# Mean squares of queries and keys in a hybrid attention layer: one float32 product replaced by two single-pass fp32r products of a rounded square and its remainder

## The reference, cut to what matters

```python
def _rms(x, w):
    xf = x.astype(jnp.float32)
    y = xf * lax.rsqrt(jnp.mean(xf * xf, axis=-1, keepdims=True) + EPS)
    return (y * w.astype(jnp.float32)).astype(x.dtype)

def _project(x, shift, scale, norm_w, w_in, q_norm_w, k_norm_w):
    h = _rms(x, norm_w) * (1 + scale) + shift
    z = h @ w_in
    q, k, v, g_att, cb, cc, ch, g_conv = jnp.split(z, idx, axis=-1)
    q = _rms(q.reshape(b, n, N_ATT_HEADS, 2, HEAD_DIM), q_norm_w)
    k = _rms(k.reshape(b, n, N_ATT_HEADS, 2, HEAD_DIM), k_norm_w)
    ...
```

## Time and profile before

| what | value |
|---|---|
| three runs, median | 1815.07 us (1813.13 to 1816.41) |
| the profiled execution's own time | 1812.12 us |
| its span, first to last instruction | 1810.3 us |
| mean granted TensorE clock | 0.973 of full speed |
| busy share of the span: PE, DVE, ACT, POOL | 93%, 58%, 44%, 42% |

### The profile page before, as it was taken

One profiled execution on the slowest core, in us unless ns is written; L12 is line 12 of the kernel. 1 busy time (PEld: TensorE's weight loads), 2 busy tenths in 40 slices (PEclk: granted clock), 3 DMA queues, 4 the chain that ended last, 5 costly groups with the idle time before them and its releaser, 6 DMA issues.

```text
span 1810.3 us, 25375 instructions
## 1 busy us (share of the span) xinstructions
PE 1684.4 (93%) x8526; PEld 1465.4 (81%) x8526; DVE 1044.8 (58%) x1393; ACT 789.7 (44%) x1659; POOL 753.8 (42%) x807
## 2 busy tenths in 40 slices
PE   4899999989999999999589999999999999669999
PEld 1688888879989989999468888888888888558889
DVE  2552887862242322422577777777777777465653
ACT  4562333330010100100288888888888888321110
POOL 0001888860000000000188888888888888200000
PEclk7899999999999999999899999999999999779999
DMA  9962222331020120200541141114011110455441
GB/s 358 292 199 85 105 92 104 105 120 40 31 87 15 41 75 30 73 20 30 141 104 30 35 91 45 33 31 106 29 35 55 56 32 12 148 178 188 166 150 46
DMA packets 131474, 163.69 MB, mean 90 GB/s; under 512 B 10464, under 2 KB 119776, under 8 KB 130272
## 3 DMA queue, kind: packets, MB, share of 16 engines
q1 hardware_dynamic: 126288, 158.61, 27.4%
q10 hardware_dynamic: 5136, 4.46, 0.7%
HBM read 112.95 MB, written 50.07 MB: 90 GB/s over the span
## 4 chain that ended last, share of the span: by engine, by line
PE 76%; DVE 10%; DMA 4%; issue 4%; SPq 2%; ACT 2%; ACTq 1%; POOL 1%; DVEq 0%; POOLq 0%
PE ps L688 38%; PE ps L839 11%; PE ps L914 10%; PE ps L828 9%; PE ps L820 4%; DVE stt L1494 3%; DVE e L1476 2%; PE ps L752 1%; DMA wad<-in_w_ada 1%; PE ps L897 1%; DMA worw<-in_w_out 1%; DVE w L1260 1%; DMA raw<-in_w_in 1%; DVE stt L1518 1%; DMA spill_cv<-scr 1%
## 5 line engine op out<-in xcount | busy, mean ns | idle before, releaser
L688 PE MATMUL ps<-hT,w 128*128 128x448 f32 (+1 forms) x3360 | 688.1, 365 | 12.6 <-DVE w L1260 12.6
L688 PEld LDWEIGHTS ps<-hT,w 128*128 128x128 f32 x3360 | 623.1, 188 | 70.9 <-issue 27.1
L1494 DVE TENSOR_REDUCE stt<-ps 128x1 f32<-128x1024 f32 x256 | 312.6, 1221 | 133.8 <-PE ps L839 131.7
L839 PE MATMUL ps<-kb,qb 128*128 (+1 forms) x1280 | 331.9, 390 | 46.4 <-ACT e L1154 23.6
L1154 ACT ACTIVATE e<-ps,stt 128x1024 f32<-128x1024 f32 x256 | 285.5, 1115 | 139.5 <-DVE stt L1494 139.3
L839 PEld LDWEIGHTS ps<-kb,qb 128*128 128x128 f32 x1280 | 204.3, 191 | 85.5 <-issue 38.2
L828 PE MATMUL ps<-at,vb 128*128 128x256 f32 x1088 | 272.2, 380 | 0.0
L644 POOL TENSOR_TENSOR stt<-stt,lamc 128x2 f32<-128x2 f32 x64 | 12.5, 195 | 579.0 <-DVE stt L1510 579.0
L828 PEld LDWEIGHTS ps<-at,vb 128*128 128x128 f32 x1088 | 203.7, 190 | 35.9 <-issue 0.2
L650 POOL TENSOR_TENSOR e<-e,stt 128x512 f32<-128x512 f32 (+1 forms) x192 | 218.5, 1138 | 5.0
L914 PE MATMUL ps<-mix,wo 128*128 128x448 f32 (+1 forms) x960 | 204.1, 372 | 7.2 <-DVE mix L1564 7.2
(11 more groups left out here) (120 smaller groups left out, 1383.5 us busy)
## 6 DMA issues: line engine op xcount, KB each, us to landing
raw<-in_w_in SPq DMA_DIRECT2D x32, 512.0 KB, 4.0
qb<-spill_q SPq DMA_DIRECT2D x256, 64.0 KB, 2.3
scr<-in_xtok SPq DMA_DIRECT2D x8, 1024.0 KB, 8.0
wad<-in_w_ada SPq DMA_DIRECT2D x4, 2048.0 KB, 17.0
scr<-in_xT SPq DMA_DIRECT2D x8, 1024.0 KB, 6.4
kb<-spill_k SPq DMA_DIRECT2D x8, 1024.0 KB, 9.8
spill_k<-scr SPq DMA_DIRECT2D x32, 224.0 KB, 2.2
spill_q<-scr SPq DMA_DIRECT2D x32, 224.0 KB, 2.2
```

What stands on the lines that cost most here:

```text
L688: mm = pe.matmul(out, slot_of(l, j), rhs_of(r, j), start=(i == 0 and j == 0), stop=(i == 2 and j == DJ - 1))
L839: mm = pe.matmul(out[:, c0 - k0:c1 - k0], qb[:, t, ver, m], keys, start=(ver == 0), stop=(ver == 1))
L1494: dve.tensor_reduce(stt[:, b, 0, 3 * m + c:3 * m + c + 1], ps[:, 2 * c:2 * c + 2, :].rearrange("p c n -> p (c n)"), AX.X, ALU.max, negate= ...
```

## The change

The square of a unit is no longer one float32 tensor that is multiplied by a float32 `blk`. ACT writes it twice from the same PSUM bank: once as fp32r into `qsh` (the rounded part, two buffers) and once as float32 into `qsq` (now a single buffer). DVE subtracts the first from the second into `qsl` (fp32r, two buffers), in a new function `square_lo`. PE multiplies `qsh` and `qsl` one after the other by `blkr`, an fp32r copy of `blk`, into the same PSUM bank. In DVE's stream `square_lo(k+1)` stands ahead of unit k's reciprocal, and `square_lo(0)` ahead of the stage; ACT's second Square of unit k waits for DVE's subtract of unit k-1, as `qsq` has one buffer. DVE makes `blkr` once, before the stage, and PE waits for it once. DVE's loop over heads 1 to 3 becomes a loop over heads 1 and 2 and a written-out last head, whose last unit has no square ahead of it. The rest moves buffers to make room: small early tensors share their place with `qsl` and `blkr`, and `qsh` lies in the scratch area.

```diff
--- before.py
+++ after.py
@@ -102,21 +102,24 @@
         taps, b_ada = small[:, 11:27], small[:, 27:51]
         c_in = small[:, 51:67]
         eps = sb("eps", [P, 1])
-        sc = sb("sc", [P, DJ, 32])
         sel = sb("sel", [P, 2])
         xss = sb("xss", [P, XN, 2])
         xsd = sb("xsd", [P, XN, 2])
         xrs = sb("xrs", [P, XN, 2])
-        modg = sb("modg", [P, 3 * P])
         mod = sb("mod", [P, 24, 2])
         mult = sb("mult", [P, DJ, 2])
-        lamv = sb("lamv", [P, 4, HD])
-        lamj = sb("lamj", [P, 2, HD])
         lamt = sb("lamt", [P, 6])
         lamc = sb("lamc", [P, 2])
         sublns = sb("sublns", [P, 1])
         qks = sb("qks", [P, 2])
         tick = sb("tick", [P, 1])
+        with ExitStack() as ectx:
+            sc = sb("sc", [P, DJ, 32], F32, ectx)
+            modg = sb("modg", [P, 3 * P], F32, ectx)
+            lamv = sb("lamv", [P, 4, HD], F32, ectx)
+            lamj = sb("lamj", [P, 2, HD], F32, ectx)
+        qsl = sb("qsl", [P, 2, GW], F32R)
+        blkr = sb("blkr", [P, P], F32R)
         cw = sb("cw", [P, 4])
 
 
@@ -134,7 +137,10 @@
                 qx = sb("qx", [P, 8, N], F32, qctx)
             w = sb("w", [P, 5, 2, DJ, P], F32R, actx)
             raw = sb("raw", [P, 2, DJ, P], F32, actx)
-            scr = sb("scr", [P, 8000], F32, actx)
+            with ExitStack() as sctx:
+                scr = sb("scr", [P, 8000], F32, sctx)
+            sb("padq", [P, 2 * T + 5 * N], F32, actx)
+            qsh = sb("qsh", [P, 2, GW], F32R, actx)
 
         with ExitStack() as bctx:
             kb = sb("kb", [P, 2, 2, KEYS], F32R, bctx)
@@ -185,7 +191,8 @@
         vout = [vhi, vlo]
 
         cosT, sinT = scr[:, 0:T], scr[:, T:2 * T]
-        qsq, qhi, qlo = ([scr[:, 2 * T + (2 * i + b) * N:2 * T + (2 * i + b + 1) * N] for b in range(2)] for i in range(3))
+        qhi, qlo = ([scr[:, 2 * T + (2 * i + b) * N:2 * T + (2 * i + b + 1) * N] for b in range(2)] for i in range(2))
+        qsq = scr[:, 2 * T + 4 * N:2 * T + 5 * N]
         qrs, qzn, qt1, qt2 = ([qx[:, 2 * i + b] for b in range(2)] for i in range(4))
 
         sig = scr[:, 0:2 * N].rearrange("p (b n) -> p b n", b=2)
@@ -229,6 +236,9 @@
         mod_mm = sem("mod_mm")
         mod_ch = sem("mod_ch")
         sq_ready = sem("sq_ready")
+        sq_hi = sem("sq_hi")
+        sq_lo = sem("sq_lo")
+        blk_ready = sem("blk_ready")
         sum_mm = sem("sum_mm")
         std_ready = sem("std_ready")
         rstd_ready = sem("rstd_ready")
@@ -745,12 +755,15 @@
                             gate_turn(g - 1)
 
 
+            pe.wait_ge(blk_ready, 1)
+
             def qk_sums(k, u):
                 n = GROUPS[u % NG][1]
-                pe.wait_ge(sq_ready, XN + k + 1)
+                bank = ps[:, 5 + (XN + u) % 2, 0:n]
+                pe.wait_ge(sq_lo, k + 1)
                 wait(pe, std_ready, XN + k - 1)
-                pe.matmul(ps[:, 5 + (XN + u) % 2, 0:n], blk, qsq[u % 2][:, 0:n], start=True, stop=True)\
-                    .then_inc(sum_mm, 1)
+                pe.matmul(bank, blkr[:], qsh[:, u % 2, 0:n], start=True, stop=False)
+                pe.matmul(bank, blkr[:], qsl[:, u % 2, 0:n], start=False, stop=True).then_inc(sum_mm, 1)
 
             def qk_unit(h, u, last=True):
 
@@ -1022,7 +1035,10 @@
                     n = GROUPS[u % NG][1]
                     act.wait_ge(z_mm, QK0 + k + 1)
                     act.wait_ge(sum_mm, XN + k - 1)
-                    act.activation(qsq[b][:, 0:n], ps[:, (QK0 + u) % BANKS, 0:n], ACT.Square).then_inc(sq_ready, 1)
+                    z = ps[:, (QK0 + u) % BANKS, 0:n]
+                    act.activation(qsh[:, b, 0:n], z, ACT.Square).then_inc(sq_hi, 1)
+                    wait(act, sq_lo, k)
+                    act.activation(qsq[:, 0:n], z, ACT.Square).then_inc(sq_ready, 1)
                 if root:
                     n = GROUPS[(u - 1) % NG][1]
                     act.wait_ge(sum_mm, XN + k)
@@ -1319,14 +1335,27 @@
                 if 2 <= g <= 4:
                     gate_add(g - 2)
             dve.wait_ge(lam_ch, 7)
-
-            def qk_unit(h, u):
+            dve.wait_ge(gate_tr, 3)
+            dve.tensor_copy(blkr[:], blk).then_inc(blk_ready, 1)
+
+            def square_lo(k, u):
+
+                n = GROUPS[u % NG][1]
+                dve.wait_ge(sq_hi, k + 1)
+                dve.wait_ge(sq_ready, XN + k + 1)
+                wait(dve, sum_mm, XN + k - 1)
+                dve.tensor_tensor(qsl[:, u % 2, 0:n], qsq[:, 0:n], f32(qsh[:, u % 2, 0:n]), ALU.subtract)\
+                    .then_inc(sq_lo, 1)
+
+            def qk_unit(h, u, ahead=True):
 
                 n = GROUPS[u % NG][1]
                 comp = 1 - u // NG
                 k = QK_UNITS * h + u
                 b = u % 2
                 rs, zn = qrs[b][:, 0:n], qzn[b][:, 0:n]
+                if ahead:
+                    square_lo(k + 1, (u + 1) % QK_UNITS)
                 dve.wait_ge(std_ready, XN + k + 1)
                 dve.reciprocal(rs, rs).then_inc(rstd_ready, 1)
                 dve.wait_ge(rstd_ready, XN + k + 1)
@@ -1343,11 +1372,14 @@
                 if u == 6:
                     w_split(QKC + 2 * h + 2, 0, 4)
 
+            square_lo(0, 0)
             for u in range(QK_UNITS):
                 qk_unit(0, u)
-            with dve.Fori(1, H) as h:
+            with dve.Fori(1, H - 1) as h:
                 for u in range(QK_UNITS):
                     qk_unit(h, u)
+            for u in range(QK_UNITS):
+                qk_unit(H - 1, u, ahead=u < QK_UNITS - 1)
             w_split(CVC + 1, 1, CV_SLOT[1])
 
 
```

## The result

The changed kernel took 1822.83 us in the median of eight runs (1820.95 to 1825.83); the kernel before, in eight runs beside it, 1815.50 us (1813.13 to 1820.05). The ratio is 1.0040 with a 95% interval of 1.0029 to 1.0052: slower by 7.3 us. 1826.7 us had been forecast, within 1812 to 1837. The profiled execution took 1820.95 us with a span of 1819.2 us.

A forecast was written before the change was run, and what follows sets the result against it. PE bounds the q/k stage, with DVE close behind; then DVE would. On DVE +0.35 +27.6 +12.0 -0.7 -27.7 gives +11.6 us; 1812.12 + 11.6 = 1823.7, plus the median's 2.95: 1826.7 us, range 1812 to 1837.

The forecast's parts named there:

- Direction and mechanism: q/k stage: subtracts overfill DVE's 27.7 us of spare time, PE's 15.6 us saved become waiting; slower, +11.6 us.
- The cost of a subtract: DVE in the q/k stage: 0.50 us plus 0.42 waiting for POOL, 0.92 each; 1.5 behind a w_split.
- The order behind a w_split: DVE and POOL, eight subtracts: POOL's waiting line 615 goes first, so each subtract costs 1.5 us, not 0.50.
- the unit that has its input ready: DVE in the q/k stage: a unit takes 4.58 us, reciprocal to reciprocal; a short one 4.04.
- Rival 4: PE in the q/k stage: new pauses lower its clock, costing up to 20 us, 1845 us; chance 0.04.
- The distance to the median: Whole kernel: the profiled execution lies 2.95 us under the median, and the forecast keeps that distance.

The follow-up runs named there:

- x1: The changed kernel with ACT's second Square written to a free PSUM bank instead of SBUF: 1804.34 us, ratio 0.9944 to the kernel before.
- x3: The changed kernel with one float32 product of the rounded part on PE, remainder not summed, Squares and subtract kept: 1823.71 us, ratio 1.0037.
- x7: The kernel before with two long-satisfied DVE waits moved from behind the reciprocal to in front of it: 1813.20 us, ratio 0.9999.

## Why the prediction came out as it did

**Direction and mechanism: right.** DVE had 27.7 us to spare, the subtracts cost more than that, and PE's saving became PE's waiting. x1 and x3 show both halves.

**The cost of a subtract: right.** Forecast were 0.92 us a subtract and 1.5 behind a w_split, 38.9 us in all. Measured: from the first reciprocal to the last w_split the changed kernel takes 396.05 - 170.72 = 225.3 us, the one before 388.33 - 170.53 = 217.8, so 7.5 more. With 27.7 - 1.0 = 26.7 us of idle time filled and 4.0 us of gaps gone (below), the 38 subtracts cost 7.5 + 26.7 + 4.0 = 38.2 us.

**The order behind a w_split: right**, POOL first; it was taken by symmetry from one row, and all eight such subtracts of the changed kernel last 1.54 to 1.57 us.

**What was mis-sized: the unit that has its input ready.** The step said 4.58 us, reciprocal to reciprocal, and took it for DVE's own load. It held 0.19 us of waiting behind the reciprocal, which I read as part of the instruction chain. The change made this vanish in 25 units, by 0.16 each: 4.0 us. Nine of the 25 are the last head's, and writing that head out is a part of the change to which the prediction gave no time. Forecast +11.6; less 4.0 for the gaps, less 0.7 for subtracts a little cheaper, less 0.2 at the start, plus 1.0 for idle time not filled: +7.7 us, as the profile has it. The row had an idle figure with DVE as its own releaser; that figure was the hint. The profiled executions are 1820.95 - 1812.12 = 8.8 us apart all the same, so part of the error was made up by the clock at the start of the convolution stage (1.6 us), which had not been forecast: that part is luck.

**Rival 4** happened, and inside the stage it did no harm. The prediction gave it 0.04, because only the long wait had lowered the clock in the trace before. But in the changed kernel the pass behind the 2.66 us wait took 6.35 us, where the next one (248.09 us) took 5.03, and the stretches below show the clock (from and to, length, busy of PE, PEld, DVE, ACT and POOL, then PEclk):

```profile
240.00:262.00 22.00, 21.26 (x96) 19.41 (x97) 21.72 (x26) 8.62 (x17) 18.93 (x17) 0.92 0.31 111
...
383.00:392.00 9.00, 4.47 (x15) 3.76 (x14) 8.72 (x11) 3.70 (x7) 7.00 (x7) 0.62 0.14 51
```

In the stage it cost nothing: no reciprocal waited. Behind the stage, where PE is the one waited for, the profiled execution lost 1.6 us to a lower clock, but x7's has the same drop, so it is not shown to come from the change. (The price of 1845 that the prediction put on this rival should be 1826.7 + 20 = 1846.7.)

**The distance to the median.** I kept the 2.95 us by which the profiled execution lay under the median. With eight runs the median of before is 1815.50, and the forecast against it would have been 1827.1; the error of some 4 us is the term above.

## What to carry to other kernels

Before an engine is given work to relieve another, add up its idle time inside the stage, not its busy share: here DVE, busy 58% of the span, had 0.7 us a unit to spare, and the work cost 1.0. Two-input elementwise work on DVE beside a busy POOL costs what it waits as well as what it runs (1.03 us instead of 0.62 here): put one input into PSUM, or put it where it starts before POOL's next operation, and look at what stands ahead of its inputs in the other engines' streams. Idle gaps that an engine seems to cause itself may be register operations between two waits; they are no fixed part of the work.

## What the runs showed of the hardware that was not expected

- A register operation between a satisfied wait and the next DVE instruction showed as 0.19 to 0.22 us of idle time, against 0.03 to 0.04 without it.
- TensorE's clock was low behind waits of 2.51, 2.66 and 2.83 us on PE (for the second, 0.92 in the mean of 22 us and a pass of 6.35 us; for the third, 0.79 in the 8 us from the wait's end), while in the kernel before a wait of 2.22 us was followed by matmuls 0.2 us apart, and in x1 one of 2.43 us by a pass of 5.13 us. What exactly separates them was not tried.
- DVE and POOL hand the memory that they share to the one that has been waiting, in both directions: DVE ahead of POOL's next operation at line 613's end, POOL ahead of DVE's next at the w_split's end (239.14), where the subtract then lasted 1.54 us.
